# Two chained transformer blocks on one core: another order in the recurrent stage, and other places of some weight splits and of a bias

## What is computed

```python
# recurrent mixer
proj = x @ w_in
q, k, v, o, ig, fg = jnp.split(proj, M_SPLITS, axis=-1)   # 512, 512, 1024, 1024, 4, 4
...
s = jnp.einsum('bhtk,bhsk->bhts', qc, kc) * d             # d: decay from the gates
...
h = num / jnp.maximum(jnp.abs(den), jnp.exp(-m_t))[..., None]
h = (h - mu) * lax.rsqrt(var + LN_EPS) * head_g           # per head
return (jax.nn.sigmoid(o) * h) @ w_out
# window attention ends in
return out @ w_o + b_o
# second block, for each mixer
x = layer_norm(DEEPNORM_ALPHA * x + mix, mix_ln_g[i], mix_ln_b[i])
x = layer_norm(DEEPNORM_ALPHA * x + jnp.square(jax.nn.relu(x @ w_up)) @ w_down, ...)
```

## Time and profile before

| | |
|---|---|
| median of 3 runs | 1734.73 us (1726.45 to 1735.23) |
| the profiled execution | 1730.97 us |
| its span, first to last instruction | 1729.2 us |
| mean granted TensorE clock | 0.981 |
| busy: TensorE, VectorE, ScalarE | 1649.7, 959.7, 773.7 us |
| read from memory | 280.46 MB, 163 GB/s over the span |

### The profile page before, as it was taken

The page is one execution under the profiler, slowest core; times in us unless marked ns, Lnnn a source line. Parts: engine busy times, 40 slices in busy tenths (PEclk is TensorE's granted clock), DMA queues, the critical chain, the costliest instruction groups (busy, mean ns, idle before and its releaser), DMA issues.

```text
span 1729.2 us, 24292 instructions
## 1 busy us (share of the span) xinstructions
PE 1649.7 (95%) x10586; PEld 1491.6 (86%) x10586; DVE 959.7 (55%) x1043; ACT 773.7 (45%) x943; POOL 44.9 (3%) x119
## 2 busy tenths in 40 slices
PE   7999998999999999999999999988999999889998
PEld 6999897789998999978899988877999877779986
DVE  5544555455445554478554454566555667755556
ACT  5434534454335544357544344324444436344442
POOL 1000000100000000010000001000000001000000
PEclk9999998999999999999999998999999999999999
DMA  6655454046554555541465554535565452365562
GB/s 233 198 192 187 155 186 167 1 137 211 187 185 158 195 196 178 183 130 49 136 217 185 186 190 141 164 97 174 181 194 192 155 177 74 126 203 186 181 199 73
DMA packets 187864, 283.57 MB, mean 164 GB/s; under 512 B 5687, under 2 KB 142510, under 8 KB 187630
## 3 DMA queue, kind: packets, MB, share of 16 engines
q1 hardware_dynamic: 184702, 271.29, 47.5%
q0 software_dynamic: 3056, 10.73, 1.9%
HBM read 280.46 MB, written 1.05 MB: 163 GB/s over the span
## 4 chain that ended last, share of the span: by engine, by line
PE 82%; DVE 9%; ACT 4%; DMA 4%; issue 2%; SPq 0%; POOL 0%; DVEq 0%; ACTq 0%
PE wk L554 13%; PE wk L556 13%; PE wk L555 13%; PE acc L554 12%; PE acc L555 12%; PE acc L556 12%; DVE weights_low L1502 3%; ACT weights_high L1166 2%; DMA weights_raw<-ffn_w_in_dram 1%; DMA weights_raw<-mlp_w_down_dram 1%; DMA weights_raw<-mlp_w_up_dram 1%; PE wk L591 1%; PE wk L801 1%; DMA weights_raw<-a_w_in_dram 1%; PE wk L793 1%
## 5 line engine op out<-in xcount | busy, mean ns | idle before, releaser
L1502 DVE TENSOR_TENSOR weights_low<-weights_raw,weights_high 128x2048 fp32r<-128x2048 f32 (+1 forms) x258 | 588.2, 2284 | 554.4 <-ACT weights_high L1166 554.3
L1166 ACT ACTIVATE weights_high<-weights_raw 128x2048 fp32r<-128x2048 f32 (+1 forms) x258 | 489.5, 1899 | 252.8 <-PE acc L556 86.3
L554 PE MATMUL wk<-turned_high,weights_high 128*128 128x256 f32 x1936 | 548.6, 283 | 0.6 <-DVE weights_low L1502 0.6
L555 PE MATMUL wk<-turned_low,weights_high 128*128 128x256 f32 x1936 | 548.2, 283 | 0.0
L556 PE MATMUL wk<-turned_high,weights_low 128*128 128x256 f32 x1936 | 548.2, 283 | 0.0
L554 PEld LDWEIGHTS wk<-turned_high,weights_high 128*128 128x128 f32 x1936 | 371.5, 192 | 3.8 <-issue 1.3
L555 PEld LDWEIGHTS wk<-turned_low,weights_high 128*128 128x128 f32 x1936 | 371.5, 192 | 2.4
L556 PEld LDWEIGHTS wk<-turned_high,weights_low 128*128 128x128 f32 x1936 | 371.6, 192 | 0.0
L554 PE MATMUL acc<-weights_high,hidden_high 128*128 128x512 f32 x616 | 243.8, 396 | 13.3 <-DVE hidden_low L1623 13.3
L555 PE MATMUL acc<-weights_low,hidden_high 128*128 128x512 f32 x616 | 242.6, 394 | 0.0
L556 PE MATMUL acc<-weights_high,hidden_low 128*128 128x512 f32 x616 | 241.8, 392 | 0.0
(11 more groups left out here) (277 smaller groups left out, 1120.3 us busy)
## 6 DMA issues: line engine op xcount, KB each, us to landing
weights_raw<-ffn_w_in_dram SPq DMA_DIRECT2D x88, 1024.0 KB, 5.1
weights_raw<-ffn_w_out_dram SPq DMA_DIRECT2D x44, 1024.0 KB, 4.9
weights_raw<-mlp_w_up_dram SPq DMA_DIRECT2D x32, 1024.0 KB, 5.5
weights_raw<-mlp_w_down_dram SPq DMA_DIRECT2D x32, 1024.0 KB, 4.9
weights_raw<-sb_w_in_dram SPq DMA_DIRECT2D x12, 1024.0 KB, 5.1
weights_raw<-a_w_in_dram SPq DMA_DIRECT2D x12, 1024.0 KB, 5.1
weights_raw<-ple_w_gate_dram SPq DMA_DIRECT2D x8, 1024.0 KB, 5.0
weights_raw<-sb_w_out_dram SPq DMA_DIRECT2D x4, 1024.0 KB, 5.1
```

What stands on the lines that cost most here:

```text
L554: nc.tensor.matmul(dst, lh, rh, start=first, stop=False)
L555: nc.tensor.matmul(dst, lh, rl, start=False, stop=False)
L1166: A(part(whi, u), part(raw, u), ACT.Copy).then_inc(high_ready, 1)
L1502: V.tensor_tensor(part(wlo, u), part(raw, u), part(whi, u).bitcast(F32), ALU.subtract).then_inc(unit_ready, 1)
```

## The change

Recurrent stage: after the gates TensorE takes queries and keys first (now U+5 to U+8), to banks 1, 2, 0 and 3 of `wk`; then one value unit, the scores, two value units, the outputs of heads 0 and 1, the last value unit, the turns of the first half, and the outputs of heads 2 and 3, which go to `wk`. VectorE copies the values by halves and normalises two heads at a time (`normalize`). The output weights come by contraction halves, and `out_product` serves this stage too; the second half is turned after the first row tile of the second column half. The places of the splits follow.

Latent and window stages: the last output unit is split before the wait for the second half of the turned rows.

Squared MLP: unit U+5 is split after the high and low halves of the hidden rows, no longer before.

`leave_norm`: after the recurrent stage only one unit of the next stage is split ahead; the second is split between the two row tiles. The bias of the window stage moves ahead of the last splits (`add_bias`).

The diff, cut ("..." stands for what is left out: semaphore names, the removed bodies of `turn_mixed` and of the old normalisation, bank numbers in the gate part):

```diff
+        def ml_out(h, t):
+            return acc[:, t, h * M_DV:(h + 1) * M_DV] if h < 2 else wk[:, h, t * M_DV:(t + 1) * M_DV]
+        def ml_den(p):
+            if p == 0:
+                return wk[:, 0:2, QB:QB + T]
+            return acc[:, 0, BANK:BANK + 2 * T].rearrange("p (h t) -> p h t", t=T)
...
-        MIXED_AT = {"mla": 0, "mlstm": 2 * T, "swa": 3 * T}
+        MIXED_AT = {"mla": 0, "mlstm": 2 * T, "swa": 4 * T}
         def mix_bank(name, b):
-            return wk[:, b, :] if name == "mlstm" else acc[:, b, 0:BANK] if b < 2 else wk[:, b - 2, :]
+            return acc[:, b, 0:BANK] if name != "mlstm" and b < 2 else wk[:, b % 2, :]
...
-                    quarters(U + 5, w_in, D)
-                    columns(U + 9, w_in, 0, 4)
-                    quarters(U + 13, a["a_w_out_2"][0])
+                    columns(U + 5, w_in, 0, 4)
+                    quarters(U + 9, w_in, D)
+                    by_rows(U + 13, a["a_w_out_2"][0])
...
+                    if name == "mlstm" and c:
+                        pe.wait_ge(ml["den_read"], 2)
                     for t in range(T):
                         mm = row_tile(U + c, acc[:, t, c * BANK:(c + 1) * BANK], 0, t, BANK)
-                    mm.then_inc(unit_done, 1)
-                    if c == 0:
-                        turn_half(name, 1)
+                        if t == T - 1:
+                            mm.then_inc(unit_done, 1)
+                        if (c, t) == ((1, 0) if name == "mlstm" else (0, 1)):
+                            turn_half(name, 1)
...
-                pe.wait_ge(ml["o_kept"], T)
-                row_product(U + 5, lambda t, c: acc[:, t, 0:BANK], halves=1)
+                group_up(U + 5, 1)
+                group_up(U + 6, 2)
                 pe.wait_ge(ml["gates_ready"], 1)
...
-                row_product(U + 7, lambda t, c: acc[:, t, BANK:D], halves=1)
+                group_up(U + 7, 0)
                 pe.wait_ge(ml["consts"], 2)
                 pe.wait_ge(ml["m_ready"], 1)
                 pe.wait_ge(ml["floor_ready"], 1)
+                pe.wait_ge(ml["q_kept"], 2)
...
-                for j, bank in enumerate((1, 2, 3, 0)):
-                    if j == 1:
-                        pe.wait_ge(ml["cols_kept"], 1)
-                    if j >= 2:
-                        pe.wait_ge(ml["bounded"], 2 * (j - 1))
-                    group_up(U + 9 + j, bank)
-                pe.wait_ge(ml["q_kept"], 2)
-                pe.wait_ge(ml["k_kept"], 2)
+                pe.wait_ge(ml["cols_kept"], 1)
+                group_up(U + 8, 3)
...
+                def v_unit(n):
+                    wait_unit(U + 9 + n)
+                    for t in range(T):
+                        mm = row_tile(U + 9 + n, acc[:, t, (n // 2) * BANK:(n // 2 + 1) * BANK], 4 * (n % 2), t, BANK)
+                    mm.then_inc(unit_done, 1)
+                pe.wait_ge(ml["o_kept"], T)
+                v_unit(0)
+                pe.wait_ge(ml["k_kept"], 2)
+                pe.wait_ge(ml["bounded"], M_HEADS)
                 for h in range(M_HEADS):
                     scores(h)
+                v_unit(1)
+                v_unit(2)
                 pe.wait_ge(ml["v_kept"], 1)
-                for h in range(M_HEADS):
-                    outputs(h)
+                outputs(0)
+                outputs(1)
+                v_unit(3)
+                turn_half("mlstm", 0)
+                pe.wait_ge(ml["v_kept"], 2)
+                outputs(2)
+                outputs(3)
...
-                if name in ("mla", "swa"):
+                if name in ("mla", "mlstm", "swa"):
...
-                split(U + 5)
+                if r == 1:
+                    split(U + 5)
                 for j in range(r):
                     act.wait_ge(hidden_turned, F + j + 1)
                     A(hTh[:, j].rearrange("p k s -> p (k s)"), wk[:, j, :], ACT.Copy).then_inc(hidden_high, 1)
+                if r == 2:
+                    split(U + 5)
...
-                split_to(U + 8)
+                split_to(U + 9)
...
+            def mlstm_stage(U, o):
+                def keep_q(j):
+                    act.wait_ge(unit_done, U + 6 + j)
+                    A(ml_q[:, 2 * j:2 * j + 2, :].rearrange("p h s -> p (h s)"), wk[:, 1 + j, :], ACT.Copy,
+                      scale=M_DK ** -0.5).then_inc(ml["q_kept"], 1)
+                def deviation(p):
+                    act.wait_ge(ml["var_ready"], p + 1)
+                    A(ml_half[:, 4 * p:4 * p + 4], ml_var[:, 4 * p:4 * p + 4], ACT.Sqrt,
+                      bias=eps[:, 2:3]).then_inc(ml["dev_ready"], 1)
+                split_to(U + 7)
                 act.wait_ge(unit_done, U + 4)
                 for t in range(T):
                     A(ml_gate[:, t, :], acc[:, t, :], ACT.Sigmoid).then_inc(ml["o_kept"], 1)
-                split_to(U + 9)
                 act.wait_ge(ml["biased"], 1)
                 A(ml_small[:, 0:16], ml_small[:, 0:16], ACT.Tanh, scale=1.0 / GATE_CAP).then_inc(ml["tanh"], 1)
                 act.wait_ge(ml["abs"], 1)
                 act.preload_act_table_set("natural_log_exp_and_others")
                 chain.link(A(ml_small[:, 16:24], ml_small[:, 16:24], ACT.Exp, scale=-1.0))
                 A(ml_small[:, 16:24], ml_small[:, 16:24], ACT.Ln, bias=1.0).then_inc(ml["log"], 1)
-                split_to(U + 11)
+                split_to(U + 8)
+                keep_q(0)
+                keep_q(1)
+                split_to(U + 9)
                 act.wait_ge(ml["m_ready"], 1)
                 A(ML_FLOOR, ML_FLOOR, ACT.Exp, scale=-1.0).then_inc(ml["floor_ready"], 1)
-                split_to(U + 13)
+                split_to(U + 10)
                 for h in range(M_HEADS):
                     act.wait_ge(ml["bounded"], h + 1)
                     A(ml_decay[:, h, :], ml_decay[:, h, :], ACT.Exp).then_inc(ml["decay_ready"], 1)
+                act.preload_act_table_set("sqrt_and_others")
                 split_to(U + 14)
-                for j in range(2):
-                    act.wait_ge(unit_done, U + 10 + j)
-                    A(ml_q[:, 2 * j:2 * j + 2, :].rearrange("p h s -> p (h s)"), wk[:, 1 + j, :], ACT.Copy,
-                      scale=M_DK ** -0.5).then_inc(ml["q_kept"], 1)
-                    split_to(U + 15)
-                act.preload_act_table_set("sqrt_and_others")
-                act.wait_ge(ml["var_ready"], 1)
-                A(ml_half, ml_var, ACT.Sqrt, bias=eps[:, 2:3]).then_inc(ml["dev_ready"], 1)
+                deviation(0)
+                keep_mixed("mlstm", o, range(2))
+                split_to(U + 16)
+                deviation(1)
...
-                split_to(U + 9)
+                split_to(U + 10)
...
-                    split_to(U + STAGE_UNITS[name] + 2)
+                    split_to(U + STAGE_UNITS[name] + (1 if name == "mlstm" else 2))
...
-                split_to(U + STAGE_UNITS[name] - 1)
+                split_to(U + STAGE_UNITS[name])
...
-                split_to(U + 9)
+            def mlstm_stage(U, outs):
+                split_to(U + 6)
...
+                def keep_k(j):
+                    dve.wait_ge(unit_done, U + 8 + j)
                     V.tensor_copy(ml_k[:, 2 * j:2 * j + 2, :].rearrange("p h s -> p (h s)"),
-                                  wk[:, (3, 0)[j], :]).then_inc(ml["k_kept"], 1)
+                                  wk[:, 3 * j, :]).then_inc(ml["k_kept"], 1)
...
+                def keep_v(c):
+                    dve.wait_ge(unit_done, U + 11 + 2 * c)
+                    n = slice(c * BANK, (c + 1) * BANK)
+                    for t in range(T):
+                        ins = V.tensor_copy(ml_v[:, t, n], acc[:, t, n])
+                    ins.then_inc(ml["v_kept"], 1)
+                def normalize(p):
+                    dve.wait_ge(ml["out_ready"], 2 * p + 2)
+                    js = range(4 * p, 4 * p + 4)
+                    for j in js:
+                        chain.count(V.bn_stats(ml_small[:, 48 + 6 * j:54 + 6 * j], ml_out(j // T, j % T)))
+                    den = ml_inv[:, 4 * p:4 * p + 4].rearrange("p (h t) -> p h t", t=T)
+                    V.tensor_scalar(den.bitcast(I32), ml_den(p).bitcast(I32), 0x7fffffff, None,
+                                    ALU.bitwise_and).then_inc(ml["den_read"], 1)
+                    dve.wait_ge(dve_chain, chain.n)
+                    dve.wait_ge(ml["den_read"], p + 1)
+                    for j in js:
+                        chain.count(V.bn_aggr(ml_small[:, 96 + 2 * j:98 + 2 * j], ml_small[:, 48 + 6 * j:54 + 6 * j]))
+                    chain.link(V.tensor_tensor(den, den, ml_cols[:, 1, :, 2 * p:2 * p + 2].rearrange("p t h -> p h t"), ALU.max))
+                    chain.link(V.reciprocal(den, den))
+                    var = ml_var[:, 4 * p:4 * p + 4].rearrange("p (h t) -> p h t", t=T)
+                    chain.link(V.tensor_tensor(var, ml_moments[:, 2 * p:2 * p + 2, :, 1], den, ALU.mult))
+                    V.tensor_tensor(var, var, den, ALU.mult).then_inc(ml["var_ready"], 1)
```

(40 more changed lines are left out.)

100 lines of the change are left out of this document (23 added, 77 removed).

## The result

| | before | after |
|---|---|---|
| median | 1732.38 us (4 runs, 1726.45 to 1735.23) | 1705.25 us (4 runs, 1704.36 to 1708.65) |
| the profiled execution | 1730.97 us | 1704.36 us |
| its span | 1729.2 us | 1702.6 us |
| mean granted clock | 0.981 | 0.986 |

The ratio is 0.9841 (95% interval 0.9824 to 0.9858); a second measurement of the changed kernel gave 0.9830 (0.9814 to 0.9846). So the change takes 27 to 30 us, 1.6 to 1.7%, off the time. The forecast was 1702 with a range of 1694 to 1718; 1705.25 is 3 us above the one and inside the other.

What follows compares the result with a forecast made beforehand. TensorE's product stream was taken as the bound, leaving only holes and half clock to win. The terms 4.1 + 9.7 + 6.0 + 3.8 + 7.7 = 31.3 us gave 1699.7 to 1703.4, forecast 1702, range 1694 to 1718.

Steps and rivals of the forecast that it cites:

- 1, latent exit: Leaving the latent stage: splitting the last output unit earlier gains 2.4 us of hole and 1.65 of half clock, 4.1 us.
- 2, recurrent stage: Recurrent stage: the new order of units removes holes and half clock, ending the output product 11.8 us sooner.
- rival D: Recurrent stage: splits wait in order, loads go one at a time, so the kernel is slower, 1745 us; chance 0.04.
- rival B: Recurrent stage gives part back: late splits make two new holes, 8 to 12 us, 1710 to 1714; chance 0.16.
- 3, its exit: Leaving the recurrent stage: first hole 1.1 us, then delays of 1.5 and 1.4; of 11.8 us gained, 9.7 remain.
- 4, openings: Squared MLP openings: moving U+5's split shrinks holes to 1.5 and 3.4 us, gaining 6.0 and 3.8 us with clock.
- 5, window exit: Leaving the window stage: earlier split and moved bias adds cut the hole to 0.8 us; 7.7 us with clock.
- Rival C: Whole kernel: no change, time won is given back because weights cannot come sooner; 1728 to 1736 us; chance 0.08.

Runs made afterwards that it cites:

- e1: The kernel before with only the openings' edit: the split of U+5 moved behind the copies of the hidden rows; 1724.85 us, ratio 0.9961.
- e6: The kernel before with the recurrent stage's part of the change alone, its exit included; 1723.23 us, ratio 0.9945.
- f2: The kernel before with the latent and window exits alone: last output unit split early, bias adds ahead of the splits; 1721.36 us, ratio 0.9928.
- e8: The changed kernel with the last output unit of the latent and window stages split late again, bias adds staying moved; 1716.02 us, ratio 0.9901.
- e4: The changed kernel with the second MLP unit behind the recurrent stage split ahead of the first add again; 1709.46 us, ratio 0.9866.
- e2: The changed kernel with the split of U+4 also moved behind the copies of the hidden rows in the squared MLPs; 1696.31 us, ratio 0.9794.
- f0: The changed kernel itself, unaltered, run again; 1703.56 us, ratio 0.9830 to the kernel before.
- e5: e2 plus U+5's split behind the copy in plain feed-forward openings and an earlier ScalarE split at the recurrent exit; 1694.19 us, second run 1694.52.
- f1: e5 with the recurrent stage's 8-column gate products interleaved with 256-column products of the first query unit, and splits earlier; 1689.20 us, ratio 0.9743.
- e7: The changed kernel with the window exit's two bias adds back between the splits and the first add; 1709.07 us, ratio 0.9864.

## Why the prediction was right

**What bounds the kernel.** It is TensorE's stream, as said. There were five places with a hole. Each was reduced by taking work out of the way of one wait, each was worth its hole and part of the half clock behind it, and they add up (e1, e6, f2).

**1, latent exit (4.1).** The mechanism holds (e8, f2): the hole went from 2.96 to 0.54. The clock's term was mis-sized. Of the half clock at 845.2 only 0.6 us could be had (turn interval 9.23 to 8.62), not 1.65. At full clock TensorE waits 0.74 us in this interval for the low copies of the turned rows, where at half clock it waited for nothing; so 0.74 of the missing 1.05 lay beside these copies. The real gain is 3.1; the trace shows 4.6 because a spell inside the heads, worth 1.6, was in the profile of before and not in that of after.

**2, recurrent stage (11.8).** From the stage's first turn to the end of the output product 129.98 became 118.10: 11.9. The layout by prices from the earlier trace rows was right in its parts. The trace of after, moved by 1.72 us so that the stage's first turns coincide, has the low halves of U+8 to U+12 and of U+14 to U+16 at 1088.6, 1096.1, 1100.8, 1108.9, 1115.0, 1132.3, 1140.0 and 1146.1. The forecast had 1088.8, 1096.4, 1101.0, 1109.0, 1115.3, 1132.6, 1140.7 and 1146.5. None is late, as the stretch 1072.6 to 1152.9 shows, so rival D (loads one at a time) and rival B (new holes) are out. The stretch holds both groups of eight turns and stood at 1.00. The Trainium skill says (TensorE: Matmul & The Clock Gate, Part 4: PE-mode transpose) that transpositions do not count as busy for the clock in the same way; no fall followed these two groups of eight. The half clock was 6.8 us long (1065.8 to 1072.6). It set in inside the gate products, 2.5 us before their end, so that 4.3 of it lay behind them, where I had 3.3.

**3, its exit (2.1 given back, 9.7 left).** There was a hole of 0.59 where I had 1.1, then 1.20 and 1.15 where I had 1.5 and 1.4. The mechanism is the forecast one. With the second unit ahead of the add the second turn is 4.85 us later (e4).

**4, openings (6.0 and 3.8).** In this pair of profiles they gave 4.8 and 5.0. That the sum is my 9.8 is luck. I took the time of U+4's load from the trace of before, once for each opening. The first load took 6.00 us there and 7.05 in after, so the hole ended at 2.48, not 1.5; the second took 7.84 there and 6.61 in after, so the hole ended at 2.05, not 3.4. For the clock of the second opening I misread a row: I had 3.1 us lost in 6.2, but the earlier trace rows has a clock of 0.77 there, which is 1.4 lost. With a spell of 3.4 us kept, as I assumed, there was nothing to win (e1), and my term of 1.4 came true only because the spell was absent in after. Whether it comes is not settled by the hole: of the ten openings in all profiles with a hole of 2.0 to 2.5 us five had 3.4 us at half clock behind it. The six with holes of 4.5 to 5.8 all had half clock, the one with 1.5 us and the eleven with less than 1 us had none. What I did not see is that the low half need not stand behind U+4 either (e2).

**5, window exit (7.7).** The hole 6.82 became 1.22 to 1.29 (e2, f0, f2); I had 0.8. In after it is 0.38; a spell at 1454.9 slowed TensorE ahead of it, as in e5 and f1, which have 0.38 too. The clock gave 1.0 (turn interval 8.39 to 7.38), not 1.75; here 0.46 us of waiting for the copies came in. The real gain is 6.5 (106.25 to 99.72); the same spell makes it 5.8 in the profile of after.

**Sum.** Without the spells in the latent heads and in the window stage the five places give 3.1 + 10.3 + 4.8 + 6.5 + 5.0 = 29.7 us against 31.3 forecast. The openings are worth less in other profiles: the first 3.4 to 3.7 by f0 and e7, the second 4.0 to 4.2 where the MLP of e6 or f2 (183.48 and 183.70 us, opening as before) stands for the old one. That makes 27 to 30, as the medians have it. The error of the forecast is that of the clock at the two exits (1.8 us in all), of the window exit's hole (0.4) and of the openings. Rival C (weights cannot come sooner) is out: in the five changed places TensorE waits for weights once, 1.2 us.

## What to carry to other kernels

Where engines work through queues in order, look at each wait of the bounding engine for the instruction that stands ahead of the awaited one and waits for something else, mostly a load. Move it behind, and ask which unit the next product really needs: at the openings another 5.1 us were still there after this change (e2). Then look at what the moved work releases: a split also frees a load buffer, so an add moved ahead of splits delays a load. Price a half clock spell by the next distance between two fixed points, not by half its length, and do not read less than 4 us from the spans of one pair of profiles: compare stage by stage, with several profiles.

## Hardware seen on the way

- The clock fell without any hole. TensorE issued products of 8 columns back to back from 1061.8, and the granted clock went from 1.00 to 0.50 at 1065.8 and came back at 1072.6, 4.3 us into the 256-column products that began at 1068.3. With the same products mixed in between 256-column ones (f1) it stayed at 1.00. All ten profiles of the new order in which they stand in a row have this spell, 6.8 or 6.9 us long.
- Spells at half clock differ between executions of the same instructions: 13.6, 17.1 or 20.5 us in the stick-breaking stage, none or 3.4 us in the latent heads, none, 3.4 or 6.8 us in the window stage.
- Three row vectors of 0.5 MB on GpSimd's queue, issued 4.3 us ahead, lengthened a 1 MB load from 5.5 to 7.05 us. With the same spacing the load took 6.55 to 7.40 us in nine profiles.
